# First network's attention on one Trainium2 core: the steps of a slot as one lump between pieces of the projections

## What is computed

```python
h = jnp.einsum('bsd,de->bse', x, w_in[l])
rq, rk, rv, rg, cq, ck, cv, dq, dk, dv, gates = jnp.split(h, splits, axis=-1)
o_a = _retention(...)          # 4 heads
o_b = _chunk_attention(...)    # 8 heads of 64, relative bias, softmax(q k + bias) v
o_c = _diff_attention(...)     # 4 heads, softmax(q0 k0) - lam * softmax(q1 k1), times v, RMS norm
g = jax.nn.sigmoid(gates + b_merge[l]).reshape(B, S, N_BRANCHES, D)
merged = (g[:, :, 0] * jnp.einsum('bse,ed->bsd', o_a, w_branch_a[l])
          + g[:, :, 1] * jnp.einsum('bse,ed->bsd', o_b, w_branch_b[l])
          + g[:, :, 2] * jnp.einsum('bse,ed->bsd', o_c, w_branch_c[l]))
x = _layer_norm(DEEPNORM_ALPHA * x + merged @ w_out[l], ln1_g[l], ln1_b[l])
# then a gated feed-forward network and a second layer norm
```

## Time and profile before

| | |
|---|---|
| median of 3 runs | 1994.32 us (1994.09 to 1995.76) |
| profiled execution, device time | 1995.39 us |
| profiled execution, span | 1993.5 us |
| PE busy | 1974.0 us, 99% |
| PE weight loads busy | 1801.5 us, 90% |
| DVE busy | 1254.2 us, 63% |
| ACT busy | 904.8 us, 45% |
| DMA | 361.84 MB, mean 182 GB/s |

### The profile page before, as it was taken

One profiled execution on the slowest core, in us unless ns is written; L12 is line 12 of the kernel. 1 busy time (PEld: TensorE's weight loads), 2 busy tenths in 40 slices (PEclk: granted clock), 3 DMA queues, 4 the chain that ended last, 5 costly groups with the idle time before them and its releaser, 6 DMA issues.

```text
span 1993.5 us, 31852 instructions
## 1 busy us (share of the span) xinstructions
PE 1974.0 (99%) x13856; PEld 1801.5 (90%) x13856; DVE 1254.2 (63%) x1785; ACT 904.8 (45%) x1202; POOL 99.3 (5%) x84
## 2 busy tenths in 40 slices
PE   8999999999999999999999999999999999999998
PEld 7888999999888999999999989799999998979997
DVE  6566656665656766655565567765566556776555
ACT  4445444444445544444444445444444444444442
POOL 0000001000100000100100020010010002001000
PEclk9999999999999999999999999999999999999999
DMA  8444466666544455796666646368657665646663
GB/s 289 165 146 148 170 211 189 199 210 191 171 167 149 141 177 197 196 264 181 180 203 188 189 151 173 106 194 259 190 169 212 189 187 148 176 106 195 187 189 106
DMA packets 421412, 361.84 MB, mean 182 GB/s; under 512 B 29392, under 2 KB 361496, under 8 KB 421272
## 3 DMA queue, kind: packets, MB, share of 16 engines
q1 hardware_dynamic: 421272, 359.80, 59.0%
HBM read 358.72 MB, written 1.05 MB: 180 GB/s over the span
## 4 chain that ended last, share of the span: by engine, by line
PE 95%; DVE 4%; ACT 1%; issue 0%; DMA 0%; DVEq 0%; SPq 0%
PE ps L217 22%; PE ps L218 22%; PE ps L219 22%; PE ps L224 8%; PE ps L226 8%; PE ps L225 8%; PE ps L1496 2%; PE ps L1604 1%; DVE hl L2009 1%; PE ps L1638 1%; DVE small L2114 0%; PE ps L1609 0%; ACT hl L1785 0%; PE ps L1676 0%; DVE er L2112 0%; DVE er L2155 0%
## 5 line engine op out<-in xcount | busy, mean ns | idle before, releaser
L2009 DVE TENSOR_TENSOR hl<-raw,hl 128x1024 fp32r<-128x1024 f32 (+1 forms) x532 | 722.6, 1391 | 387.0 <-ACT hl L1785 385.9
L217 PE MATMUL ps<-xt,hl 128*128 128x256 f32 (+1 forms) x2672 | 754.2, 282 | 0.0
L218 PE MATMUL ps<-xt,hl 128*128 128x256 f32 (+1 forms) x2672 | 746.2, 279 | 0.0
L219 PE MATMUL ps<-xt,hl 128*128 128x256 f32 (+1 forms) x2672 | 745.8, 279 | 0.0
L1785 ACT ACTIVATE hl<-raw 128x2048 fp32r<-128x2048 f32 (+1 forms) x337 | 613.7, 1829 | 217.9 <-PE ps L226 157.5
L217 PEld LDWEIGHTS ps<-xt,hl 128*128 128x128 f32 (+1 forms) x2672 | 500.9, 187 | 5.4 <-issue 2.3
L218 PEld LDWEIGHTS ps<-xt,hl 128*128 128x128 f32 (+1 forms) x2672 | 501.1, 188 | 3.1
L219 PEld LDWEIGHTS ps<-xt,hl 128*128 128x128 f32 (+1 forms) x2672 | 500.8, 187 | 0.2
L224 PE MATMUL ps<-hl,o 128*128 128x512 f32 x656 | 261.3, 398 | 0.0
L226 PE MATMUL ps<-hl,o 128*128 128x512 f32 x656 | 259.0, 395 | 0.0
L225 PE MATMUL ps<-hl,o 128*128 128x512 f32 x656 | 258.8, 395 | 0.0
(11 more groups left out here) (197 smaller groups left out, 1578.9 us busy)
## 6 DMA issues: line engine op xcount, KB each, us to landing
raw<-in_w_in SPq DMA_DIRECT2D x83, 1024.0 KB, 5.0
raw<-in_w_ffn_in SPq DMA_DIRECT2D x88, 512.0 KB, 5.1
raw<-in_ffn_gate SPq DMA_DIRECT2D x88, 512.0 KB, 3.9
raw<-in_ffn_up SPq DMA_DIRECT2D x88, 512.0 KB, 5.2
raw<-in_ffn_down SPq DMA_DIRECT2D x44, 1024.0 KB, 5.1
raw<-in_w_ffn_out SPq DMA_DIRECT2D x22, 1024.0 KB, 5.0
raw<-in_w_out SPq DMA_DIRECT2D x24, 512.0 KB, 4.7
raw<-in_w_branch_a SPq DMA_DIRECT2D x8, 1024.0 KB, 5.0
```

The lines of the kernel that those rows point to most:

```text
L217: e.matmul(out, l[0], r[0], start=start, stop=False)
L218: e.matmul(out, l[0], r[1], start=False, stop=False)
L219: return e.matmul(out, l[1], r[0], start=False, stop=stop)
L2009: e.tensor_tensor(lo[:, c], m["raw"][:, k % NRAW, 0:n][:, c], hi[:, c].bitcast(F), ALU.subtract).then_inc(s.low.up(("low", k), *([("low", ...
```

## The change

A second way to run the slots, `lumps`, is added, and both attentions of the first network use it in place of `slots`. It takes the same steps in the same order, but adds their costs up and yields once per slot, so that `mix` puts no piece of the projections between them. Only a step that yields `IDLE`, or a slot without S (where `PART` is yielded), ends a lump early. The second network's attention keeps `slots`.

```diff
+    def lumps(tasks, order):
+
+        for n in range(len(tasks) + 2):
+            lump = 0
+            for x in order:
+                if 0 <= n + x < len(tasks):
+                    cost = next(tasks[n + x])
+                    while cost is IDLE:
+                        if lump:
+                            yield lump
+                            lump = 0
+                        yield IDLE
+                        cost = next(tasks[n + x])
+                    lump += cost
+                elif x == 0:
+                    yield lump + PART
+                    lump = 0
+            if lump:
+                yield lump
+
...
-            yield from slots([task(i, jp) for i in range(2) for jp in range(2)], (-1, 0, -2, -1))
+            yield from lumps([task(i, jp) for i in range(2) for jp in range(2)], (-1, 0, -2, -1))
...
-            yield from slots([task(i, jp) for i in range(2) for jp in range(2)], (0, -2, -1))
+            yield from lumps([task(i, jp) for i in range(2) for jp in range(2)], (0, -2, -1))
```

## The result

| | before | after |
|---|---|---|
| median of the runs, us | 1994.76 (6 runs) | 2003.95 (6 runs) |
| lowest and highest, us | 1994.09 to 1995.9 | 2003.17 to 2004.66 |
| span of the profiled execution, us | 1993.5 | 2002.7 |
| PE busy, us | 1974.0 | 1977.0 |
| mean granted clock | 0.999 | 0.998 |

The ratio is 1.0045, with a 95% interval of 1.0034 to 1.0055: 9.2 us slower. The forecast was 1999.9, the range ended at 2003.5. The direction and the place were right; the size was not.

A forecast was written before the change was run, and what follows sets the result against it. PE, busy for 1974.0 of 1993.5 us, was taken to bound the kernel. The terms 5.6 + 1.6 - 1.0 + 0.2 - 0.8 gave 5.6 us, so 1999.9 us on the median, range 1996.9 to 2003.5.

The forecast's parts named there:

- The order of the lumps: Both attentions: slots begin where they began, S keeps its place, V and turn move up behind S, no lump cut.
- the signs named: Profile after: waits at turn0 and behind V1, none at V2, 30 islands, full clock, busy time down about a microsecond.
- Step 1: First attention, turn0 behind S1: PE waits 2.8 us for DVE's scaling, 5.6 us for two layers.
- rival (c): Behind the turn0 waits the clock falls, PE works slowly for 8 us each; 8 us more, 2008 us; chance 0.05.
- Step 2: First attention, turn2 behind S3 and V1: PE waits 0.8 us a layer for DVE, 1.6 us for two.
- Step 3: First attention, V2 no longer waits for turn2's copies: 0.48 us a layer back, about 1.0 us for two.
- Step 4: Second attention, slot 3: the norm after V1 delays DVE's weight pair; PE loses 0.1 us a layer, 0.2 for both.
- Step 5: Both attentions: twenty fewer islands save 2.0 us, 24 new neighbours inside lumps cost at 0.05 each; 0.8 us saved.
- Rival (a): Island returns and neighbours decide, sum as low as 2.6 us, 1996.9 us; chance 0.19 within 0.2%, 0.04 faster.
- rival (b): DVE's backlog at slot 3 of both attentions: steps 2 and 4 at upper ends, 2002.3 us; chance 0.12.

The follow-up runs named there:

- The run with slot 1 opened: The whole change, but in the first attention a yield between S1 and turn0 lets the projections back in: 1996.59 us, ratio 1.0007.
- The run with the second attention alone: Lumps in the second attention only, the first attention keeping its slots as in the kernel before: 1995.06 us, ratio 1.000.
- the eleven matmuls: The whole change plus eleven unused 512-column matmuls on PE between S1 and turn0 in the first attention: 2001.48 us, ratio 1.0028.
- the earlier scaling: The whole change, with DVE's scaling in the first attention moved to the end of S, ahead of the weight halves: 1998.0 us, ratio 1.0015.
- the same edit with slots: The kernel before, slots kept, with DVE's scaling in the first attention moved to the end of S: 1998.18 us, ratio 1.0016.
- The versions with turn and V one slot later: Kernel before, first attention's turn two and V three slots behind S: in lumps 1991.94 us, repeated 1992.69 us; with slots 1993.45 us.
- the longer wait: The whole change plus six further reciprocals on DVE ahead of the scaling of slot 1 in the first attention: 2007.25 us, ratio 1.0061.

## Why the prediction was wrong, step by step

- **The order of the lumps** was right: S of every slot kept its place, and PE shows S1 turn0, S2 V0 turn1, S3 V1 turn2, V2 turn3 next to each other. There are 15 islands a layer in place of 25, and the idle time of PE rises by 6.2 us, as forecast. Of the signs named, two failed: the granted clock does not stay at full, and the busy time of PE rises by 3.0 us and does not fall by one.
- **Step 1, the wait** was right: 2.73 us of idle time in both layers against 2.8. The run with slot 1 opened shows that this one place carries the loss: 7.4 us by the medians, and 1.7 us a layer came back as another wait.
- **What failed is the price of that wait.** The sum took it as idle time alone, and rival (c), a clock that falls, had a chance of 0.05. It happened. The 18 projections took 5.78 us in layer 0 and 5.92 in layer 1 (631.20 to 637.12) in place of 4.31, so 1.5 and 1.6 us, about 3.1 in all. That is the step that failed: a term of 3.1 us that the sum put at nothing. Rival (c) had the mechanism and sized it too high, at 8 us, from the start of the run, which is no measure for it (see the last section). The argument against it, that shorter waits of before left the pace alone, said nothing on a wait more than twice as long as any in the middle of that trace. The Trainium skill ("TensorE: Matmul & The Clock Gate", Part 1) says that the clock is gated after idle time, and the trace agrees: 0.50 behind 2.73 us.
- **Step 2** was right: 0.81 and 0.80 us behind V1 against 0.8.
- **Step 3** was right: no wait at V2.
- **Step 4** was right in place and size: the norm goes ahead of the pair, and PE loses some 0.2 us against 0.1.
- **Step 5** was about right as a sum. From S0 of the first to S0 of the second attention before took 52.35 us and after 56.68. The waits and the clock come to 2.73 + 1.5 + 0.8 - 0.48 = 4.55 against these 4.33, so the islands save 0.2; the second attention is 0.2 us longer, which the gap of step 4 explains, and its islands save nothing. That is some 0.4 us for two layers against 0.8. The run with the second attention alone bears it out, with a ratio of 1.000. Rival (a) falls. The price of 0.17 us for a new change of mode did not come at S then V, the pair for which no row had a price: S2 gives way to V0 after 1.06 us (139.39 to 140.45), and before it gave way to the projections after 1.07.
- **The sum.** 5.6 as forecast, and 3.1 for the clock, is 8.7; the rest to 9.2 is the islands' smaller gain (0.4 us) and the 0.1 us a layer more of step 4. With the clock held at full by the eleven matmuls the change costs 0.28% (0.18 to 0.38), as much as was forecast: the rest of the sum holds.
- **The range.** Its upper end lay 9.2 us above the base of 1994.32 us, and 9.2 us is what was measured on a base of 1994.76. That the time came so close to the end is luck: the end stood for rival (b). The range took in the upper end of each step by itself, and not of all together, which is 12.5 us.
- Rival (b), the backlog, did not come with this change: no wait at the projections beyond those 0.2 us. It is what the earlier scaling ran into. The rival of that run had DVE blocked by the exponentials, but not the place: DVE lost 1.0 to 1.2 us before each scaling, and its rotations, not its weight halves, came late. For the same edit with slots no rival of mine had it.

One thing stays open in part. The versions with turn and V one slot later gain 2 to 3.4 us by the medians; the intervals of the ratios leave gains of only 0.4 to 1.4 us possible. From S0 of layer 0 to S0 of layer 1 PE took 493.16 us before, so the profiled executions gain 1.26 us there with slots and 1.62 and 1.71 with lumps. Of this 0.48 is the wait at V2 and 0.25 lies behind one turn of eight blocks of `xs` (1.07 us to the next projection before, 0.82 in all three). The distances from one projection to the next add up to nearly the same (450.96 us before, 450.73 to 450.87 after), so that the rest, some 0.3 us with slots and 0.8 with lumps, lies at the islands. Why the turn of `xs` gains stays open.

## What to carry to other kernels

A step moved up behind its neighbour in the order of one engine is only as good as the distance to what it reads: look in the other engines' rows for when its input is finished, and price the cover that falls away. On the matrix engine, price a wait of the length seen here, 2.7 us and more in a full stream, twice: as idle time and as half pace behind it. Waits of up to 1.68 us cost only themselves here. Filling the wait with matmuls of no use was faster than leaving it. Where steps are to stand together, stagger them by a slot more, so that each finds its input made in an earlier slot.

## What the runs showed of the hardware

The granted clock stayed at 1.00 behind waits of 1.04 and 1.68 us and fell to 0.50 behind 2.73 us in both layers. It stayed there for a little over 3 us of full work and cost 1.5 to 1.6 us; behind 4.01 us the cost was 2.5 and 1.8. Behind 2.73 us it fell only after PE had taken up its work again, in both layers, so that the slow matmuls need not be the first ones behind the wait; in the wait of 4.01 us it had fallen before PE went on.

At the start of the run before, the wide matmuls come every 0.43 us too, up to 13.38 us, behind waits of 5.32 and 1.26 us. The window there gives a full clock all the same:

```profile
10.80:13.30 2.50, 2.50 (x7) 1.98 (x6) 1.93 (x3) 1.81 (x2) 0.00 (x0) 1.00 1.06 385
```

Eleven of the thirteen profiled executions start like this. In the other two, the longer wait and the slots with the earlier scaling, the wide matmuls come every 0.23 us from the second one on, behind waits for the input of 5.02 and 5.4 us. So at the start the spacing tells the pace and the clock column does not, and a wait there was not followed by a slow stretch in every execution.

Changing the kind of matmul inside a lump cost about as much as entering it from the projections in one place and nothing in another. In the second attention of layer 0 the two mask matmuls ahead of turn0 took 0.23 us to the next instruction in place of 0.15 ahead of projections, as the trace of after shows at 189.85 us; entering S1 of the first attention took 0.32 us from the last projection in place of 0.23 (129.20 to 129.52). From S2 to V0 it cost nothing (1.06 us against 1.07).
